# Down projections of four feed-forward blocks: first two weight tiles taken chunk by chunk together

## Chip, core and metric

The kernel runs on one core of a Trainium2 chip (trn2). The metric is device time in microseconds (us) of one execution, lower is better.

## What is computed

A two-layer transformer block with context tokens, followed by a second block. The change touches only the feed-forward part, which stands four times in the program (two layers, two halves each):

```python
def swiglu(x, w_gu, w_down):
    gt, up = jnp.split(x @ w_gu, 2, axis=-1)
    return (jax.nn.silu(gt) * up) @ w_down

def half_ffn(h, g, shift, scale, gate, w_gu, w_down):
    return h + 0.5 * gate * swiglu(norm_mod(h, g, shift, scale), w_gu, w_down)
```

The model width is 1024 and the feed-forward width 2816. There are 512 tokens and 256 context tokens; the first three feed-forward parts work on all 768, the last on 512.

## The kernel before

**Tiles.** Activations lie transposed, features on the 128 partitions and tokens along the free axis. A *tile* is 128 output features; a *chunk* is 128 input features of it. Every matrix product of the kernel is a *stage* of such tiles in one long list, numbered through (`plan`, L44). The weights of a tile come by DMA into one of four `raw` slots. ScalarE (ACT) rounds them to `wh` (`split_hi`, L309) and VectorE (DVE) writes the rest to `wl` (`split_lo`, L316). `wh` and `wl` have **two slots each**, taken in turn, so `split_hi` of tile n waits until TensorE (PE) has finished tile n-2:

```python
def w_slot_free(n):
    return n + 1
...
act.wait_ge(tile_done, w_slot_free(n))
```

The count `tile_done` stands at n+3 once tile n is done. A chunk is three products (high by high, high by low, low by high), each over 512 and then, with 768 tokens, 256 columns: six matmuls on L325, or three with 512 tokens. A tile has its own 1024 columns of PSUM, four of them in turn.

**A feed-forward part.** Its width is cut in two halves, a and b, of eleven 128-wide pieces. Each half is an *up* stage (22 tiles of 8 chunks: gate and up tiles in turn) and a *down* stage (8 tiles of 11 chunks). There are so eight down stages: four parts, halves a and b. For each pair of up tiles, ACT takes silu of the gate tile (L519), and DVE multiplies by the up tile (L546), rounds the product to `hidh` (L550) and writes the rest to `hidl` (L552), which raises `hid_done` by one. `hidh` and `hidl` piece q is what chunk q of the down stage streams.

**Order around a down stage.** Each engine has a program written out by hand. Let u be the last up tile, and d0 to d7 the down tiles.

- PE (`ffn_pe`, L502; `products`, L319): tiles of the up stage; a wait until `hid_done` has counted all eleven pieces (L507); then d0, d1, ... one after the other. Before each tile PE waits for its `wl` and for its PSUM (`weights`, L331).
- ACT (`act_tiles`, L355): in its turn for tile n it first splits the weights of tile n+1, then does its own work for tile n. In a down stage of half b that own work is the square of residual row n for the next norm (L415), which waits until DVE has added tile n to `h`.
- DVE (`dve_tiles`, L364): in its turn for tile n it first does `split_lo` of tile n+1, then its own work for tile n. In the turn of u that is L546, L550, L552. In the turns of the down stage it is the add of the tile to `h` (L394).

So both split engines handle d0's weights while u is multiplied, and d1's after u is done.

`products` already has a second way to begin a stage (`chunk_ready`, from L342): it waits for the weights of **both** first tiles, and then for each chunk q calls `chunk_ready(q)` and multiplies chunk q of the first tile and chunk q of the second. The stages that follow a norm are begun so, the up stages of half a and `ev_in` among them; they are called *head pairs* below.

Of the kernel before, what the change touches and what calls it, by code (L numbers as in the profile page):

```python
# [66 lines left out]
def build(nc, t):  # L67
# [9 lines left out]
    with ctx:  # L77
# [8 lines left out]
        def sb(name, at, shape, dt=f32):  # L86
            return nc.alloc_sbuf_tensor_at(name, [P] + list(shape), dt, offset=at)

        def words(*shape):
            return 4 * int(np.prod(shape))  # L90
# [49 lines left out]
        hidh = sb("hidh", R_AT, [JA, T], f32r)  # L140
        hidl = sb("hidl", R_AT + words(JA, T), [JA, T], f32r)
# [88 lines left out]
        def S(name):  # L230
            if name not in made:
                made[name] = ctx.enter_context(nc.semaphore(name))
            return made[name]
# [8 lines left out]
        def lo_ready(n):  # L242
            return n + 5
# [7 lines left out]
        def psum_free(n):  # L251
            return n + 1
# [9 lines left out]
        def segs(tokens):  # L262
            return [(0, TX)] if tokens == TX else [(0, TX), (TX, T)]
# [20 lines left out]
        def run_tiles(eng, stage, one, done=0):  # L284


            b = stage.first
            for k in range(done, stage.head):
                one(b + k, k, b + k, None)
            if stage.loops:  # L290
                with eng.Fori(0, stage.loops) as i:
                    for c in range(stage.head, stage.head + 4):
                        one(i * 4 + (b + c), i * 4 + c, b + c, i)
            for k in range(max(done, stage.head + 4 * stage.loops), stage.tiles):
                one(b + k, k, b + k, None)
# [23 lines left out]
        def products(pe, stage, xh, xl, chunk_ready=None, then=None):  # L319


            def chunk(c, q):
                for j, (w, x) in enumerate(((wh, xh), (wh, xl), (wl, xh))):
                    for s, e in segs(stage.tokens):
                        last = nc.tensor.matmul(  # L325
                            psum[:, (c % 4) * 1024 + s:(c % 4) * 1024 + e],
                            w[:, c % 2, q * P:(q + 1) * P], x[:, q, s:e],
                            start=(q == 0 and j == 0), stop=(q == stage.chunks - 1 and j == 2))
                return last

            def weights(n):  # L331
                pe.wait_ge(w_lo, lo_ready(n))
                pe.wait_ge(drained, psum_free(n))

            def one(n, k, c, i):
                weights(n)
                for q in range(stage.chunks):
                    last = chunk(c, q)
                last.then_inc(tile_done, 1)
                if then:  # L340
                    then(k)

            if chunk_ready:
                pair = (stage.first, stage.first + 1)
                for n in pair:
                    weights(n)
                for q in range(stage.chunks):
                    chunk_ready(q)
                    for n in pair:
                        last = chunk(n, q)  # L350
                        if q == stage.chunks - 1:
                            last.then_inc(tile_done, 1)
            run_tiles(pe, stage, one, done=2 if chunk_ready else 0)
# [79 lines left out]
        def norm_pe(pe, k, tokens):  # L433


            pe.wait_ge(n_add, KD * (k + 1))
            for a in range(tokens // P):
                last = nc.tensor.matmul(psum[:, NPS[k] + a:NPS[k] + a + 1], scr[:, SQ_ALL, a * P:(a + 1) * P],
                                        ones[:, 0:1], start=True, stop=True)
            last.then_inc(n_sum, 1)  # L440
            pe.wait_ge(n_r, k + 1)
            for a in range(tokens // P):
                last = nc.tensor.matmul(psum[:, NPS[k] + a * P:NPS[k] + (a + 1) * P],  # L443
                                        ncol[:, a:a + 1].to_broadcast([P, P]), ident[:], start=True, stop=True)
            last.then_inc(n_spr, 1)
# [33 lines left out]
        def after_norm(pe, k):  # L479
            return lambda q: pe.wait_ge(n_z, KD * k + q + 1)  # L480


        silu_done, hid_hi, hid_done = S("silu_done"), S("hid_hi"), S("hid_done")
# [9 lines left out]
        def ffn_parts(f):  # L493
            return [(ST[f"ffn{f}_up_a"], ST[f"ffn{f}_down_a"], f * NJ),
                    (ST[f"ffn{f}_up_b"], ST[f"ffn{f}_down_b"], f * NJ + JA)]
# [6 lines left out]
        def ffn_pe(pe, f):  # L502
            k = NORM_OF_FFN[f]
            norm_pe(pe, k, ffn_parts(f)[0][0].tokens)
            for up, down, pairs in ffn_parts(f):
                products(pe, up, zh, zl, after_norm(pe, k) if pairs == f * NJ else None)
                pe.wait_ge(hid_done, pairs + up.tiles // 2)  # L507
                products(pe, down, hidh, hidl)

        def ffn_act(act, f):  # L510
            k, layer, s = NORM_OF_FFN[f], f // 2, 2 * (f % 2)
# [1456 lines left out]
        @block.tensor  # L1968
        def _(pe):
            pe.sem_inc(tile_done, 2)  # L1970
            pe.sem_inc(drained, 4)
            start_pe(pe)
            ffn_pe(pe, 0)
            even_pe(pe)
            ffn_pe(pe, 1)
            ffn_pe(pe, 2)
            odd_pe(pe)
            ffn_pe(pe, 3)
            dn_pe(pe)
            swa_pe(pe)  # L1980
            tail_pe(pe)
# [143 lines left out]
```

## Time and profile before

| | us |
|---|---|
| median of 3 runs | 4123.52 (4123.34 to 4126.46) |
| span of the profiled execution, first to last instruction | 4120.1 |
| PE busy in it | 3838.0 (93%) |
| DVE busy | 1719.9 (42%) |
| ACT busy | 1130.2 (27%) |
| mean granted PE clock | 0.952 of full speed |

The profile gives one execution by its span; the time of that execution outside the span is not listed apart. The median of the runs is 3.4 us above the span. The granted clock is given as a share: 1.00 is 2.4 GHz and 0.50 is 1.2 GHz, and a value between them is a stretch that holds some of both. Matmuls of 512 and 256 columns that follow each other are merged in the timeline (x2).

### The profile page before, as it was taken

The page shows a single profiled execution, that of the slowest core. Times are in us where ns is not written, and L with a number is a line of the kernel's source. Part 1 is how long each engine was busy: PE and PEld are TensorE (multiplying, and loading weights), DVE is VectorE, ACT ScalarE, POOL GpSimd, SP SyncE. Part 2 cuts the span into 40 slices and gives each one's busy share as a digit, 9 for nine tenths or more (in the row PEclk, how much of TensorE's full clock was granted, in tenths as well). Part 3 has the DMA queues.
Part 4 walks back from the last instruction along what each step waited for, and adds up shares of the span by engine and source line. Part 5 has one row for each costly group of instructions (what it writes and reads, how often), then busy time and mean ns, then how long its engine had stood idle before and what let it go on. Part 6 is the DMA issues. An engine that isn't in the chain of part 4 may idle for free.

```text
span 4120.1 us, 48230 instructions
## 1 busy us (share of the span) xinstructions
PE 3838.0 (93%) x20346; PEld 3154.8 (77%) x20346; DVE 1719.9 (42%) x2308; ACT 1130.2 (27%) x1468; POOL 15.8 (0%) x33
## 2 busy tenths in 40 slices
PE   8999999998789999999999989999998978888898
PEld 3368888887677888887888878777887777666677
DVE  6853222333764222223322244564334654444434
ACT  6741111123443111113111131443223321222232
POOL 0000000000000000000000000000000000000000
PEclk9999999998899999999999999899999987999999
DMA  9931112110001111211211212012232200111122
GB/s 367 340 119 63 65 57 75 57 59 21 4 16 52 64 64 60 71 54 51 71 52 61 70 58 80 21 45 83 93 101 79 77 1 27 46 47 45 48 76 88
DMA packets 64686, 301.67 MB, mean 73 GB/s; under 512 B 7472, under 2 KB 7664, under 8 KB 59664
## 3 DMA queue, kind: packets, MB, share of 16 engines
q1 hardware_dynamic: 61776, 286.89, 20.4%
q0 software_dynamic: 2752, 12.49, 0.8%
q8 instruction: 122, 2.00, 0.2%
q14 instruction: 36, 0.29, 0.0%
HBM read 297.25 MB, written 2.10 MB: 73 GB/s over the span
## 4 chain that ended last, share of the span: by engine, by line
PE 86%; DVE 9%; ACT 3%; issue 2%; DMA 1%; DVEq 0%; POOL 0%; ACTq 0%; SPq 0%
PE psum L325 69%; PE psum L627 5%; PE psum L937 2%; PE psum L760 2%; PE psum L954 1%; PE psum L945 1%; DVE nmx L1001 1%; PE psum L773 1%; DMA adaw<-in_ada_w 1%; PE psum L1393 1%; ACT scr L454 0%; DVE ev_s L998 0%; PE psum L443 0%; PE psum L1402 0%; DVE wl L316 0%
## 5 line engine op out<-in xcount | busy, mean ns | idle before, releaser
L325 PE MATMUL psum<-zh,wh 128*128 128x512 f32 (+1 forms) x3728 | 1124.6, 358 | 64.9 <-DVE zl L473 29.2
L325 PE MATMUL psum<-zh,wl 128*128 128x512 f32 (+1 forms) x3728 | 1118.7, 357 | 0.0
L325 PE MATMUL psum<-zl,wh 128*128 128x512 f32 (+1 forms) x3728 | 1117.6, 357 | 0.0
L316 DVE TENSOR_TENSOR wl<-raw,wh 128x1024 fp32r<-128x1024 f32 (+2 forms) x383 | 485.6, 1268 | 653.1 <-ACT wh L309 652.3
L325 PEld LDWEIGHTS psum<-zh,wh 128*128 128x128 f32 x3728 | 617.4, 191 | 176.8 <-issue 41.7
L309 ACT ACTIVATE wh<-raw 128x1024 fp32r<-128x1024 f32 (+2 forms) x383 | 416.4, 1089 | 1075.1 <-PE psum L325 1073.5
L325 PEld LDWEIGHTS psum<-zh,wl 128*128 128x128 f32 x3728 | 616.6, 190 | 106.0
L325 PEld LDWEIGHTS psum<-zl,wh 128*128 128x128 f32 x3728 | 616.2, 191 | 102.3
L325 PE MATMUL psum<-hidh,wh 128*128 128x512 f32 x1232 | 342.1, 347 | 20.2 <-DVE hidl L552 20.2
L325 PE MATMUL psum<-hidl,wh 128*128 128x512 f32 x1232 | 342.9, 348 | 0.0
L325 PE MATMUL psum<-hidh,wl 128*128 128x512 f32 x1232 | 340.4, 346 | 0.0
L394 DVE SCALAR_TENSOR_TENSOR h<-psum,mod,h 128x512 f32<-128x512 f32 (+1 forms) x136 | 82.0, 637 | 507.1 <-PE psum L325 507.1
L546 DVE TENSOR_TENSOR scr<-scr,psum 128x768 f32<-128x768 f32 (+1 forms) x88 | 78.1, 887 | 400.5 <-PE psum L325 400.5
L325 PEld LDWEIGHTS psum<-hidh,wh 128*128 128x128 f32 x1232 | 195.2, 190 | 53.3 <-DVE hidl L552 23.0
L519 ACT ACTIVATE scr<-psum 128x768 f32<-128x768 f32 (+1 forms) x88 | 66.8, 759 | 578.5 <-PE psum L325 578.5
L325 PEld LDWEIGHTS psum<-hidh,wl 128*128 128x128 f32 x1232 | 196.3, 190 | 31.4
L325 PEld LDWEIGHTS psum<-hidl,wh 128*128 128x128 f32 x1232 | 196.4, 190 | 30.0
L673 DVE TENSOR_TENSOR adal<-adaw,adah 128x2048 fp32r<-128x2048 f32 x72 | 163.9, 2290 | 54.4 <-ACT adah L653 54.3
L653 ACT ACTIVATE adah<-adaw 128x2048 fp32r<-128x2048 f32 x72 | 137.1, 1908 | 41.6 <-PE psum L627 26.2
L415 ACT ACTIVATE scr<-h 128x768 f32<-128x768 f32 (+1 forms) x56 | 43.8, 783 | 380.1 <-DVE h L394 380.1
L627 PE MATMUL psum<-adah,scch 128*2 128x512 f32 x288 | 114.8, 399 | 17.5 <-DVE adal L673 17.5
L627 PE MATMUL psum<-adah,sccl 128*2 128x512 f32 x288 | 114.1, 396 | 0.0
(365 smaller groups left out, 3229.0 us busy)
## 6 DMA issues: line engine op xcount, KB each, us to landing
adaw<-in_ada_w SPq DMA_DIRECT2D x36, 2048.0 KB, 9.5
raw<-in_wup_a SPq DMA_DIRECT2D x88, 512.0 KB, 3.3
raw<-in_wup_b SPq DMA_DIRECT2D x88, 512.0 KB, 3.3
raw<-in_wdn_a SPq DMA_DIRECT2D x32, 704.0 KB, 4.0
raw<-in_wdn_b SPq DMA_DIRECT2D x32, 704.0 KB, 4.1
raw<-in_w_sw SPq DMA_DIRECT2D x36, 512.0 KB, 3.3
raw<-in_od_in SPq DMA_DIRECT2D x16, 512.0 KB, 3.3
raw<-in_w_ga SPq DMA_DIRECT2D x16, 512.0 KB, 3.3
```

What stands on the lines that cost most here:

```text
L309: nc.scalar.activation(wh[:, c % 2, 0:w], raw[:, c % 4, 0:w], ACT.Copy).then_inc(w_hi, 1)
L316: nc.vector.tensor_tensor(wl[:, c % 2, 0:w], raw[:, c % 4, 0:w], wh[:, c % 2, 0:w], ALU.subtract).then_inc(w_lo, 1)
L325: last = nc.tensor.matmul(psum[:, (c % 4) * 1024 + s:(c % 4) * 1024 + e], w[:, c % 2, q * P:(q + 1) * P], x[:, q, s:e], start=(q == 0 and ...
L394: last = nc.vector.scalar_tensor_tensor(h[:, k, s:e], a, col, h[:, k, s:e], ALU.mult, ALU.add)
L415: nc.scalar.activation(scr[:, c % 2, 0:tokens], h[:, c, 0:tokens], ACT.Square).then_inc(n_sq, 1)
L519: nc.scalar.activation(scr[:, (c - up.first) // 2 % 2, 0:tok], acc(c, tok), ACT.Silu).then_inc(silu_done, 1)
L546: nc.vector.tensor_tensor(p, scr[:, b:b + 1, 0:tok], acc(c, tok).rearrange("p (a n) -> p a n", a=1), ALU.mult).then_inc(drained, 2)
L627: last = nc.tensor.matmul(psum[0:2, i % 4 * 512:i % 4 * 512 + 512], x[:, q, :], w, start=q == 0 and n == 0, stop=q == KD - 1 and n == 2)
L653: nc.scalar.activation(adah[:, j % 3], adaw[:, i % 3, half], ACT.Copy).then_inc(ada_hi, 1)
L673: nc.vector.tensor_tensor(adal[j % 3][:], adaw[:, i % 3, half], adah[:, j % 3], ALU.subtract).then_inc(ada_lo, 1)
L760: last = nc.tensor.matmul(psum[:, c:c + gr.heads], gr.sq[:, it.k % 2, a * P:(a + 1) * P], gr.pick(), start=True, stop=True)
L937: last = nc.tensor.matmul(u.scores(c, w), q, k, start=True, stop=True)
```

## The change

Each down stage is begun as a head pair. The one wait for all eleven pieces is gone, and chunk q waits for piece q.

```diff
--- before.py
+++ after.py
@@ -504,8 +504,7 @@
             norm_pe(pe, k, ffn_parts(f)[0][0].tokens)
             for up, down, pairs in ffn_parts(f):
                 products(pe, up, zh, zl, after_norm(pe, k) if pairs == f * NJ else None)
-                pe.wait_ge(hid_done, pairs + up.tiles // 2)
-                products(pe, down, hidh, hidl)
+                products(pe, down, hidh, hidl, lambda q: pe.wait_ge(hid_done, pairs + q + 1))
 
         def ffn_act(act, f):
             k, layer, s = NORM_OF_FFN[f], f // 2, 2 * (f % 2)
```

Lines below this one move up by one: the `hidl` write is L552 before and L551 after.

PE's program at the end of tile d0 of the first down stage, before the change (66 matmuls stand between one wait for weights and the next):

```order
1508 L325 MATMUL psum<-hidh,wl 128x512
1509 L325 MATMUL psum<-hidh,wl 128x256
1510 L325 MATMUL psum<-hidh,wh 128x512 [waits drained,w_lo]
1511 L325 MATMUL psum<-hidh,wh 128x256
1512 L325 MATMUL psum<-hidl,wh 128x512
```

Behind d0's last chunk stands the wait for d1's `wl`. In the changed kernel that place (row 1510) is in the middle of the pair and has no wait. The waits for both tiles' weights stand at row 1444, and from there on every twelfth matmul waits for its piece; this is PE at the end of chunk 0 of d1:

```order
1454 L325 MATMUL psum<-hidh,wl 128x512
1455 L325 MATMUL psum<-hidh,wl 128x256
1456 L325 MATMUL psum<-hidh,wh 128x512 [waits hid_done]
1457 L325 MATMUL psum<-hidh,wh 128x256
1458 L325 MATMUL psum<-hidl,wh 128x512
```

Chunk 1 of d0 now follows chunk 0 of d1, and the last chunk of d0 stands one chunk before the end of the pair.

DVE's program around the same boundary is the same in both (this is the changed kernel):

```order
151 L316 TENSOR_TENSOR wl<-raw,wh 128x1408 [waits w_hi]
152 L545 TENSOR_TENSOR scr<-scr,psum 128x768 [waits silu_done,tile_done]
153 L549 CAST hidh<-scr 128x768 [waits drained]
154 L551 TENSOR_TENSOR hidl<-scr,hidh 128x768 [waits hid_hi]
155 L316 TENSOR_TENSOR wl<-raw,wh 128x1408 [waits w_hi]
156 L394 SCALAR_TENSOR_TENSOR h<-psum,mod,h 128x512 [waits tile_done]
157 L394 SCALAR_TENSOR_TENSOR h<-psum,mod,h 128x256
158 L316 TENSOR_TENSOR wl<-raw,wh 128x1408 [waits w_hi]
```

Row 151 is d0's `wl`, rows 152 to 154 the last piece of the hidden values, row 155 d1's `wl`, rows 156 and 157 the add of d0, row 158 d2's `wl`. ACT's program is unchanged too; in a down stage of half b (the first of them here) it is, in both kernels:

```order
196 L309 ACTIVATE wh<-raw 128x1408 [waits tile_done,raw_loaded0]
197 L309 ACTIVATE wh<-raw 128x1408 [waits tile_done,raw_loaded1]
198 L415 ACTIVATE scr<-h 128x768 [waits drained]
199 L309 ACTIVATE wh<-raw 128x1408 [waits tile_done,raw_loaded2]
200 L415 ACTIVATE scr<-h 128x768 [waits drained]
```

These are `wh` of d0, `wh` of d1, the square of row 0, `wh` of d2, the square of row 1.

## Rows read from the trace of the kernel before

**Rows 1.** The page: busy time and share of the engines, and the chain's shares.

```profile
PE 3838.0 (93%) x20346; PEld 3154.8 (77%) x20346; DVE 1719.9 (42%) x2308; ACT 1130.2 (27%) x1468; POOL 15.8 (0%) x33
...
PE 86%; DVE 9%; ACT 3%; issue 2%; DMA 1%; DVEq 0%; POOL 0%; ACTq 0%; SPq 0%
```

**Rows 2.** Waits: engine, line, waited for; us in total, times, longest.

```profile
PE psum L325 <- DVE hidl L552: 20.2, 8, 2.7
```

**Rows 3.** Timeline at the first down stage: start us, us, engine, line, operation, count.

```profile
442.71 0.95 DVE L546 TENSOR_TENSOR scr<-scr,psum 128x768 f32<-128x768 f32 x1 [4.64 <-PE psum L325]
442.71 1.38 ACT L309 ACTIVATE wh<-raw 128x1408 fp32r<-128x1408 f32 x1 [6.30 <-PE psum L325]
...
444.29 0.96 DVE L552 TENSOR_TENSOR hidl<-scr,hidh 128x768 fp32r<-128x768 f32 x1
445.17 1.62 DVE L316 TENSOR_TENSOR wl<-raw,wh 128x1408 fp32r<-128x1408 f32 x1
...
445.30 0.97 PE L325 MATMUL psum<-hidh,wh 128*128 128x512 f32 x2 [2.69 <-DVE hidl L552]
```

**Rows 4.** Timeline at the end of the head pair of ev_in.

```profile
850.63 2.03 ACT L309 ACTIVATE wh<-raw 128x1024 fp32r<-128x1024 f32 x2 [5.12 <-PE psum L325]
...
851.07 0.50 PE L325 MATMUL psum<-zh,wl 128*128 128x512 f32 x2
851.73 1.23 DVE L316 TENSOR_TENSOR wl<-raw,wh 128x1024 fp32r<-128x1024 f32 x1 [0.19 <-ACT wh L309]
...
853.09 0.49 PE L325 MATMUL psum<-zh,wh 128*128 128x512 f32 x1 [1.51 <-DVE wl L316]
```

**Rows 5.** Timeline in the first down stage of half a, d0 just done.

```profile
458.62 1.14 DVE L394 SCALAR_TENSOR_TENSOR h<-psum,mod,h 128x512 f32<-128x512 f32 x2 [11.83 <-PE psum L325]
...
458.68 1.38 ACT L309 ACTIVATE wh<-raw 128x1408 fp32r<-128x1408 f32 x1 [14.59 <-PE psum L325]
...
460.09 1.63 DVE L316 TENSOR_TENSOR wl<-raw,wh 128x1408 fp32r<-128x1408 f32 x1 [0.33 <-ACT wh L309]
```

**Rows 6.** Timeline in the first down stage of half b, d0 just done.

```profile
737.87 1.14 DVE L394 SCALAR_TENSOR_TENSOR h<-psum,mod,h 128x512 f32<-128x512 f32 x2 [12.00 <-PE psum L325]
...
739.04 0.84 ACT L415 ACTIVATE scr<-h 128x768 f32<-128x768 f32 x1 [15.87 <-DVE h L394]
...
739.79 1.36 ACT L309 ACTIVATE wh<-raw 128x1408 fp32r<-128x1408 f32 x1
...
741.19 1.63 DVE L316 TENSOR_TENSOR wl<-raw,wh 128x1408 fp32r<-128x1408 f32 x1 [2.18 <-ACT wh L309]
```

**Rows 7.** The same in the last down stage, 512 tokens, half b.

```profile
3113.34 0.75 DVE L394 SCALAR_TENSOR_TENSOR h<-psum,mod,h 128x512 f32<-128x512 f32 x1 [6.33 <-PE psum L325]
3116.06 1.63 DVE L316 TENSOR_TENSOR wl<-raw,wh 128x1408 fp32r<-128x1408 f32 x1 [1.97 <-ACT wh L309]
```

**Rows 8.** Windows of 3.4 us after PE's short gaps: busy (x), granted clock, DMA share, GB/s.

```profile
274.38:277.78 3.40, 3.40 (x11) 0.55 0.50 154
445.30:448.70 3.40, 3.40 (x11) 0.51 0.25 65
...
1760.84:1764.24 3.40, 3.40 (x19) 1.00 0.27 65
...
3105.53:3108.93 3.40, 3.40 (x15) 1.00 0.24 60
```

**Rows 9.** Windows around a long gap between two stages of 512 tokens.

```profile
3920.00:3924.05 4.05, 4.05 (x18) 1.00 0.00 0
3924.05:3927.92 3.87, 0.00 (x1) 0.88 0.01 2
3927.92:3933.80 5.88, 5.88 (x14) 0.50 0.50 161
```

**Rows 10.** Timeline of PE within a head pair; 265.72 begins a chunk.

```profile
265.37 0.51 PE L325 MATMUL psum<-zh,wl 128*128 128x512 f32 x2
265.72 0.52 PE L325 MATMUL psum<-zh,wh 128*128 128x512 f32 x2
```

## Prediction

> **What bounds the kernel now.** I read the page's busy times and the chain of work that ended last first. PE is busy 93% of the span and the chain is 86% PE [rows 1], so a microsecond in which PE stands still beside these stages is a microsecond of the result, and so is one in which its clock is halved. DVE at 42% and ACT at 27% have room on average; what counts is where they answer late. The list of waits then says what the removed wait is worth at most: PE stood 20.2 us in all before the eight down stages, released each time by the last write of `hidl` [rows 2]. The timeline of the first such place shows what else happens in that gap [rows 3]. The last up tile u is seen done at 442.71. DVE multiplies, rounds and writes the rest, done at 445.25, and PE starts at 445.30 after 2.69 us. ACT splits d1's weights from 442.71, because only then is their slot free, and DVE cannot write d1's `wl` before 445.17, since the three hidden operations stand ahead of it in its program.
>
> **The first gap: longer by one weight split.** The change removes the wait for the last piece, and puts in its place a wait for d1's `wl` before the first matmul of the pair. On DVE that write is behind the hidden values: it starts at 445.17 and takes 1.62 us [rows 3], to 446.79. PE follows a `wl` write by 0.12 us (852.96 to 853.09 [rows 4]), so it starts at 446.91, not 445.30: **+1.6 us** in place of any gain. The waits of the chunks for their own pieces never bind, because the last piece is there 1.6 us before PE starts; the 20.2 us stay. DVE's order and width are the same in all eight stages (1408 wide in each), so 8 x 1.6 = 12.9 us.
>
> **The second gap: new, behind the pair.** d2's weights need the slot of d0. Before, d0 ended a whole tile ahead of d1's end, 66 matmuls or 11.8 us at 3.40/19 = 0.179 us each [rows 8], which covers the split. Now d0 ends one chunk before d1. The head pair of `ev_in` shows this gap at 1024 columns [rows 4]: tile 0 seen done at 850.63, the last matmul over at 851.57 (0.94 to 1.0 us later), `wl` of the third tile at 852.96, PE on at 853.09, idle 1.51 us. A down tile is wider. After d0 is seen done, ACT starts 0.06 later and takes 1.38, and `wl` ends at 461.72, 3.10 after 458.62 [rows 5]; with 0.12 it is 3.22, less the 1.0 us of d1's last chunk: **2.2 us** in half a. In half b ACT has the square of row 0 ahead of d2's `wh`, and it waits for DVE's add: done at 737.87, square at 739.04, `wh` at 739.79, `wl` at 741.19 to 742.82 [rows 6]. That is 4.95 + 0.12 - 1.0 = **4.1 us**. Before, this chain lay under tile d1. With 512 tokens a chunk is three matmuls of 4.05/18 = 0.225 us [rows 9], so only about 0.64 us is covered: half b is (3117.69 - 3113.34) + 0.12 - 0.64 = 3.8 us [rows 7], and half a 3.22 - 0.64 = 2.6 us. Sum: 3 x 2.2 + 2.6 + 3 x 4.1 + 3.8 = 25.3 us. Tile d3 does not inherit it: its split needs d1, done before d2 starts, and has d2's own length for cover. Both engines have no more work than before, and DMA is not on this path.
>
> PE's idle time added: 12.9 + 25.3 = **38.2 us**.
>
> **The clock after a gap.** This I read by windows. In the 3.4 us after the gap at 445.30 the granted clock was 0.51 and 11 matmuls ran; after that at 1760.84 it was 1.00 and 19 ran [rows 8]. Such a low stretch costs 3.4 x (1 - 11/19) = 1.4 us by the count, 3.4 x 0.49 = 1.7 by the clock; I take 1.5. There are twelve gaps of 2.0 to 2.7 us between tile products (before the eight down stages and behind the head pairs of the four up stages); nine are followed by a low stretch, three by a clock of 1.00 (1760.84, 3105.53 and one more; first, last and two between in [rows 8]), and of the eight down stages five are low. So the kernel pays 5 x 1.5 = 7.5 us at these places now. A longer gap: the one of 3.87 us is followed by 5.88 us at 0.50 in which 14 matmuls ran [rows 9]; at 0.225 us they would take 3.15, so it cost 2.7 us. The changed kernel has 12 gaps of 3.6 to 4.3 us (the first gap grows from 2.69 to 4.3, with 512 tokens from 2.0 to 3.6; and the four second gaps of half b). No down stage of before has such a gap. Its price lies between 1.5 and 2.7 us; I take the middle, 2.1, since the nearest rows are one at each end. Four second gaps of 2.2 to 2.6 us pay 1.5 us in nine cases of twelve. That is 12 x 2.1 + 4 x 9/12 x 1.5 - 7.5 = **22.2 us**.
>
> The Trainium skill (TensorE: Matmul & The Clock Gate, section HAM oscillation — how this bites in real kernels) says that short bursts of matmuls with waits between them pay the fall of the clock at each wait anew. By that rule, taken strictly, each of my sixteen gaps would pay, and the four at 9/12 would add 1.5 us in all; the trace shows three of twelve short gaps that did not.
>
> **Sum.** 4120.1 + 38.2 + 22.2 = 4180.5 us of span. The median of the runs stands 3.4 us above the span of the profiled execution, and I add that: **4184 us**, about 1.5% more than 4123.5. The idle part is firm to some 2 us. The clock part is, with 1.5 for each long gap and none for the four short ones, 10.5 us, and with 2.7 and all four, 30.9 us. So the forecast's own range is 4170 to 4195.
>
> **Rivals.**
>
> *Weight loads come into the open.* Each chunk's first matmul now waits on a count, 10 more of them in each stage, 80 in all. The Trainium skill (TensorE: Matmul & The Clock Gate, section Step-by-step: what each phase is for) says that weight loads are pulled ahead of running matmuls. If a wait stopped that, a load of 3154.8/20346 = 0.155 us [rows 1] would lie bare at each, 12 us, and the time would be 4196. Against it: in a head pair, which has the same waits, two matmuls start every 0.35 us, at a chunk's start as well [rows 10], as in a stretch without waits (3.40/19 x 2 = 0.36) [rows 8].
>
> *Only the first gap grows.* If d0's completion came early enough for the second gap to hide, only 12.9 us and about 10 us of clock would be left: 4146. For it speaks nothing but that ACT and DVE are idle then; `ev_in` shows the opposite, with a narrower split [rows 4].
>
> *Only the second gap counts,* if DVE wrote d1's `wl` ahead of the hidden values. Then the first gap keeps its length and the time is near 4123.5 + 25.3 + 12 = 4161. The timeline's order speaks against it.
>
> *Faster.* One mechanism would do it: the splits of d1 and of d2 run ahead of PE, as if the weights had a slot more. It decides at the slot: if d1's split starts 1.38 + 1.62 + 0.12 = 3.1 us before u is done [rows 3, 4], and d2's before d0 is, the first gap is gone with its clock, -20.2 - 7.5 = -28 us, and the time is 4096. ACT started d1's split at 442.71, the same instant at which DVE saw u done [rows 3], so the slot binds.
>
> *The change does not do what it says.* It does begin the stages in pairs; but the wait for each chunk's own piece is covered by the later wait for weights. This is part of the forecast. The pairing would be without effect only if both gaps were hidden: 4124.
>
> **Chances.** The forecast 0.86; loads in the open 0.04; first gap only 0.04; second gap only 0.04; faster 0.01; no effect 0.01. The range of 8 in 10 is 4167 to 4200. It takes in the clock's two prices, the 2 us of the idle part and the loads in the open. About 0.2% (8 us) is what a measurement of this kernel can tell from no change; faster by more than that 0.01, within it 0.01, slower 0.98.
>
> **What would show it.** In the changed profile PE should wait for no `hidl` at all at the eight down stages, but for DVE's `wl` L316, eight times 4.3 us (3.6 with 512 tokens). Sixteen waits of PE on `wl` should be new. Behind each pair, 22 to 24 us after its start (15 with 512 tokens), PE should stand 2.2 us in half a and 4.1 in half b, and in half b the chain should run through the add L394, the square L415, `wh` and `wl`. The mean clock should fall below 0.952, and the busy time of DVE and ACT should stay. I am wrong if PE starts the pair as `hidl` is done, if there is no gap behind the pair, or if the clock's part is outside 10 to 31 us.

## Result and the profile after

The changed kernel takes 4195.2 us (median of 4 runs, 4190.0 to 4200.1) where the kernel before takes 4125.0 beside it: a ratio of 1.018, with a 95% interval of 1.016 to 1.020. Forecast were 4184 us and a range of 4167 to 4200. A later comparison on another occasion (`after_again`, below) gave 1.016 (1.012 to 1.019); two of the 17 runs of the kernel before in that later comparison took 7.7 and 13.8 ms, and no median or ratio here counts them. The profiled execution has a span of 4198.3 us, 78.2 more than the 4120.1 of before, at a mean granted clock of 0.944 (0.952 before).

The page of the changed kernel; beside [rows 1] PE's busy time has grown by 42 us though it runs the same 20346 matmuls, and DVE and ACT are as they were:

```profile
PE 3880.2 (92%) x20346; PEld 3185.5 (76%) x20346; DVE 1719.2 (41%) x2308; ACT 1129.5 (27%) x1468; POOL 15.8 (0%) x33
```

The waits of PE. No wait for `hidl` is left (20.2 us in [rows 2]). The wait for `wl` stood in 14 places before:

```profile
PE psum L325 <- DVE wl L316: 23.6, 14, 5.5
```

It has sixteen places more now:

```profile
PE psum L325 <- DVE wl L316: 81.3, 30, 4.8
```

The chain at the first down stage. The `hidl` write now is followed by d1's `wl`, and PE starts when that is done, 4.38 us after it stopped (2.69 in [rows 3]):

```profile
445.57 0.97 DVE scr L545
...
446.56 0.57 DVE hidh L549
...
447.16 0.96 DVE hidl L551
448.12 1.54 DVE wl L316
449.66 0.20 issue
449.86 2.26 PE psum L325 x6
```

The chain behind the pair in a half a, a gap of the kind that `ev_in` had in [rows 4]: d2's `wh` as soon as d0 is done, then d2's `wl`, then PE.

```profile
474.55 1.39 ACT wh L309
...
475.96 1.64 DVE wl L316
...
477.64 1.56 PE psum L325 x7
```

And in a half b, with the add (L394) ahead of ACT's square (L415), and `wh` and `wl` behind it:

```profile
765.17 1.15 DVE h L394 x2
...
766.35 0.02 ACT scr L415
766.37 0.73 issue
767.10 1.37 ACT wh L309
...
768.49 1.64 DVE wl L316
770.13 0.04 issue
770.17 1.01 PE psum L325 x2
```

Windows of the three gaps, of what follows them, and of one long gap in the last part (busy, count, granted clock, DMA share, GB/s). They answer to [rows 8] and [rows 9]:

```profile
445.48:449.86 4.38, 0.00 (x0) 0.84 0.01 2
449.86:455.31 5.45, 5.45 (x17) 0.50 0.40 132
475.49:477.64 2.15, 0.00 (x0) 1.00 0.00 0
477.64:481.04 3.40, 3.40 (x15) 0.73 0.67 210
766.19:770.17 3.98, 0.00 (x1) 0.90 0.00 0
770.17:776.16 5.99, 5.99 (x19) 0.50 0.47 134
2979.33:2983.04 3.71, 0.00 (x0) 1.00 0.37 147
2983.04:2986.44 3.40, 3.40 (x15) 1.00 0.63 212
```

The gap before a stage is 4.38 us five times and 4.41 once in the parts of 768 tokens, and 3.7 twice with 512. Behind the pair it is 2.15 three times and 2.5 in half a, and 4.0 three times and 3.75 in half b.

**Where the 78 us are.** I take each of the four feed-forward parts from the end of its first up stage to the end of its last down stage. In the first part that is 442.61 to 819.45 before and 445.48 to 841.82 after, 19.5 us more; the others give 20.4, 13.4 and 15.0, in sum 68.3 us. Of these 38.2 us are idle time. The other 30.1 are, by the windows and the experiments below, the lower clock, 20.7 us, and a slower pace of the products, 7.9 us; 1.5 us stay without a cause. Ten us lie outside these four stretches: 2.9 up to the first down stage, whose up stage ran at the slower pace, some 2.6 between the parts and just behind the last, and 4.3 behind 3188 us in the second block. There PE is busy 4.5 us longer with the same work, at a mean granted clock of 0.91 where it was 0.92, and idle no longer than before; why the clock was lower there stays open.

### The profile page after: what moved, and what is told of

The parts are those of the page before. It is cut to its first block, busy times and chain, and to the rows that moved or that the text cites. A ratio compares the mean times of both kernels' runs of the same rounds, so it can differ in the third digit from the quotient of the medians.

```text
span 4198.3 us, 48230 instructions
## 1 busy us (share of the span) xinstructions
PE 3880.2 (92%) x20346; PEld 3185.5 (76%) x20346; DVE 1719.2 (41%) x2308; ACT 1129.5 (27%) x1468; POOL 15.8 (0%) x33
## 4 chain that ended last, share of the span: by engine, by line
PE 85%; DVE 9%; ACT 3%; issue 2%; DMA 1%; DVEq 0%; ACTq 0%; POOL 0%; SPq 0%
PE psum L325 68%; PE psum L626 4%; PE psum L936 2%; PE psum L759 2%; PE psum L953 1%; PE psum L944 1%; DVE nmx L1000 1%; DVE wl L316 1%; PE psum L772 1%; DMA adaw<-in_ada_w 1%; PE psum L1392 1%; ACT wh L309 1%; ACT scr L454 0%; DVE ev_s L997 0%; PE psum L443 0%
## 5 line engine op out<-in xcount | busy, mean ns | idle before, releaser
L325 PE MATMUL psum<-zh,wh 128*128 128x512 f32 (+1 forms) x3728 | 1130.2, 360 | 64.2 <-DVE zl L473 29.2
L325 PE MATMUL psum<-hidh,wh 128*128 128x512 f32 x1232 | 352.2, 356 | 58.5 <-DVE wl L316 58.5
L325 PE MATMUL psum<-hidh,wl 128*128 128x512 f32 x1232 | 348.9, 353 | 0.0
L394 DVE SCALAR_TENSOR_TENSOR h<-psum,mod,h 128x512 f32<-128x512 f32 (+1 forms) x136 | 82.0, 637 | 571.4 <-PE psum L325 571.4
L415 ACT ACTIVATE scr<-h 128x768 f32<-128x768 f32 (+1 forms) x56 | 43.8, 783 | 415.9 <-DVE h L394 415.9
```

What stands on the lines that cost most here:

```text
L325: last = nc.tensor.matmul(psum[:, (c % 4) * 1024 + s:(c % 4) * 1024 + e], w[:, c % 2, q * P:(q + 1) * P], x[:, q, s:e], start=(q == 0 and ...
L394: last = nc.vector.scalar_tensor_tensor(h[:, k, s:e], a, col, h[:, k, s:e], ALU.mult, ALU.add)
L415: nc.scalar.activation(scr[:, c % 2, 0:tokens], h[:, c, 0:tokens], ACT.Square).then_inc(n_sq, 1)
```

## Experiments

Each ratio is to the kernel before, run beside it on the same chip, with its 95% interval. 1% is 41 us. An edit is shown against the changed kernel, the first one against the kernel before.

**Chunk waits alone.** Twice, under two labels. A new argument of `products` calls the wait in the first tile of a stage that is not a pair:

```diff
             def one(n, k, c, i):
                 weights(n)
                 for q in range(stage.chunks):
+                    if piece and i is None and k == 0:
+                        piece(q)
                     last = chunk(c, q)
...
-                pe.wait_ge(hid_done, pairs + up.tiles // 2)
-                products(pe, down, hidh, hidl)
+                products(pe, down, hidh, hidl, piece=lambda q: pe.wait_ge(hid_done, pairs + q + 1))
```

> Chunk waits alone, tiles one after the other as before the change. Theory (a pair is what costs, chunk waits are harmless): d0's weights are ready 4 us before the last up tile ends and pieces 0 to 9 are done, so the eight gaps of 2.0 to 2.7 us (20.2 us) go, with the 7.5 us that the clock lost after five of them: about 4125 - 28 = 4097 us, PE waits for hidl 0 us. Rival 1 (a wait in front of a chunk bares a weight load of 0.155 us, 88 times): 4111. Rival 2 (the last piece binds in any order): 4125.

Measured: 0.992 (0.989 to 0.995), 4093.3 us beside 4121.8. That is 28.5 us less by the medians and 34 by the ratio (22 to 47). PE goes from the up stage into the down stage without a stop:

```profile
445.78 0.51 PE L325 MATMUL psum<-zh,wl 128*128 128x512 f32 x2
446.12 0.51 PE L325 MATMUL psum<-hidh,wh 128*128 128x512 f32 x2
446.48 0.53 PE L325 MATMUL psum<-hidl,wh 128*128 128x512 f32 x2
```

All eight gaps are gone with the low clock behind them, and the size fits the theory. The pair is the cost of the change; the chunk waits are its better half, and 88 of them bare no weight load. The stretch that begins at 273.80 in `chunk_again` (see the pace, below) has 22 of these waits in it and still ran at the faster of the two paces, 534.33 us for 3072 products; 22 bare loads of 0.155 us would have added 3.4. The Trainium skill (TensorE: Matmul & The Clock Gate, Step-by-step: what each phase is for) has the weight loads pulled ahead of running matmuls; by these numbers that holds across a wait that is already met.

> The kernel with chunk waits alone once more, timed beside the others. Theory: about 28 us under before (ratio 0.993), with no gap at the eight down stages; its three stretches of 3072 products draw their pace anew, each worth 10 us, so single runs spread over some 30 us. Rival (the pace of this kernel is fixed at 0.353): the three stretches are at 0.353 again and the spread is under 10 us.

Measured: 0.991 (0.989 to 0.994), 4090.4 us beside 4124.7, 34 us less; single runs from 4067.4 to 4096.6. The eight gaps are absent again, and one of the three long stretches ran at the faster pace, where in the first trace of this kernel none did.

**The pair with one wait.**

```diff
-                products(pe, down, hidh, hidl, lambda q: pe.wait_ge(hid_done, pairs + q + 1))
+                products(pe, down, hidh, hidl, lambda q: pe.wait_ge(hid_done, pairs + up.tiles // 2) if q == 0 else None)
```

> The pair, with one wait for all eleven pieces ahead of it. Theory: the wait for d1's wl ends 1.6 us after the last piece, so the chunk waits do nothing: same time as the changed kernel, 4195 us within 8. Rival (the chunk waits save part of the gap, which would be longer without them, or cost weight loads): 4210 or more, or 4183 or less.

Measured: 1.015 (1.010 to 1.019), 63.8 us over before, and PE waits 81.0 us for `wl` in 30 places and never for `hidl`, as in the changed kernel. The chunk waits do nothing behind a pair that waits for d1's weights.

**d0 done six chunks early.** The steps of a pair are written out, and the two tiles part before the end:

```diff
+                lead = stage.chunks - ahead
+                steps = [(q, n) for q in range(lead) for n in pair] + [(q, n) for n in pair for q in range(lead, stage.chunks)]
+                for q, n in steps:
+                    if n == pair[0]:
+                        chunk_ready(q)
+                    last = chunk(n, q)
+                    if q == stage.chunks - 1:
+                        last.then_inc(tile_done, 1)
```

Down stages take ahead=6; with the default of 1 the head pairs are as they were.

> The pair is interleaved for its first 5 chunks only; then d0's last 6 and then d1's last 6, so d0 ends six chunks (6.2 us, 4.1 with 512 tokens) before d1. Theory: the second gap (24.7 us in all) goes with its low clock (some 12 us), the first gap stays at 4.4 us: about 4195 - 37 = 4158 us, still slower than before by 33. Rival (the second gap has another cause, as the add to h or the next tile's transfer): 4190 or more.

Measured: 1.005 (1.003 to 1.007), 4145.4 beside 4121.8. In the profile every gap behind a down pair is gone and those ahead of the stages stay (4.38 to 4.41, and 3.7). Against `pair_one_wait` (63.8 us over before, in the same comparison) the second gap was worth some 40 us, where 37 were expected, and the first some 24. That the second is the slot's release is shown by both: the edit moved only the moment at which d0 ends, and the chains above go from that moment to d2's `wh` and `wl` and so to PE (in half b by way of the add and the square, see `square_late`).

**Filling the first gap of the pair.** PE multiplies d0's first chunks while it waits for d1's weights, each as a product of its own that the real one overwrites:

```diff
                 for n in pair:
                     weights(n)
+                    if fill and n == pair[0]:
+                        for q in range(fill):
+                            chunk(n, q, alone=True)
```

> While PE waits for d1's weights it multiplies d0's first 4 chunks (5 with 512 tokens) into the same PSUM, to be overwritten: 4.2 us of work in a wait of 4.4. Output unchanged. Theory (the low clock after the first gap is a cost of its own, about 2.1 us each): the clock stays at 1.00 after it, -17 us, about 4178 us. Rival 1 (the clock is no part of it): 4195. Rival 2 (the filling runs past the wait): 4200.

Measured: 1.010 (1.007 to 1.013), 4169.0 beside 4121.8; 16.6 us under `pair_one_wait` of the same comparison, where 17 were expected. The wait ended within 0.2 us of where it did, and the clock stays up from the stretch before to well behind it (windows, as above; the same at all eight stages):

```profile
444.00:449.00 5.00, 4.94 (x29) 1.00 0.17 41
449.00:455.00 6.00, 6.00 (x37) 1.00 0.22 90
```

Behind its gap the changed kernel ran 17 matmuls in 5.45 us, this one 37 in 6.00. Only the filling differs from the changed kernel, so the low clock after a gap is shown to be a cost of its own. The size is less firm: the 95% intervals of the two ratios just overlap. The two profiled spans are 8.4 us apart (4180.6 and 4172.2), and 2680 more products of the filled one ran at the slower pace (below), 8.8 us: without the pace it is 17.2.

**Filling the gap of the kernel before.**

```diff
                 weights(n)
+                if fill and i is None and k == 0:
+                    for q in range(2):
+                        chunk(c, q, alone=True)
+                    fill()
```

> The kernel before, with d0's first 2 chunks multiplied into their PSUM and overwritten, between the wait for d0's weights and the wait for all eleven pieces: 2.1 us of work (1.4 with 512 tokens) in a wait of 2.7 (2.0). Output unchanged. Theory: the wait ends when it did, and the clock stays up at all eight stages: -7.5 us against before. Rival (a short gap's low clock is chance and costs nothing on average): 0. The draw of the pace (see below, 0.347 or 0.353 us for two products) moves either by some 5 us.

Measured: 0.997 (0.995 to 0.999), 4113.8 beside 4129.2; by the ratio 13 us less, with an interval of 5 to 21. The 7.5 us at which I priced the five low stretches lie inside it, and no low stretch is left at any of the eight stages, where 0.6 us of idle time stays of each gap. PE does 2 us of useless work per stage here (1.4 with 512 tokens) and the kernel is faster for it.

**The order on DVE.** d1's `wl` ahead of the last `hidl` write, once with chunk waits and once with one wait:

```diff
+                    if i is None and j == up.tiles - 1:
+                        split_lo(dve, n + 2, c + 2, None)
                     dve.wait_ge(hid_hi, pair + 1)
                     nc.vector.tensor_tensor(ol, p, oh, ALU.subtract).then_inc(hid_done, 1)
```

(and the down stage's first turn no longer does that split).

> The changed kernel, with DVE's write of d1's wl moved ahead of the last hidl write (after the multiply and the rounding). Theory (the first gap ends with d1's wl, in DVE's order): wl starts as the rounding ends, 1.55 us after u, takes 1.62, so the gap is 3.4 us instead of 4.4 (3.3 instead of 3.7 with 512 tokens), -6.8 us in all and perhaps 2 of clock; the last piece comes 0.9 us after PE has started, and only the chunk waits allow that. Rival (PE cannot start before the last piece): the gap stays 4.3, 0 us.

Measured: 1.010 (1.008 to 1.012), 4164.1 beside 4124.7. The chain at the first down stage; PE starts with the last piece not yet written (it is done at 448.02):

```profile
445.06 0.56 DVE hidh L549
445.62 1.55 DVE wl L316
447.17 0.20 issue
447.37 2.04 PE psum L325 x5
```

The gap is 3.39 us six times and 3.34 twice, as expected. The time was not: some 9 us less than the changed kernel were expected, and the ratios say 24 to 33. In the traces, with the slower pace taken off, the spans differ by 18 and 22 us. The gaps are 6.7 of that. Most of the rest is clock: the mean granted clock is 0.947 here and 0.944 and 0.945 in the two traces of the changed kernel. Not all of it lies behind these gaps, and why there is less low clock elsewhere stays open.

> split_first with one wait for all pieces ahead of the pair. Theory: PE starts when hidl is done, 4.3 us after u: time of the changed kernel, about 8 us over split_first. Rival (chunk waits have no value in any order): the time of split_first.

Measured: 1.013 (1.011 to 1.016), 4179.8 beside 4124.7. PE starts only behind `hidl`, with a gap of 4.19:

```profile
443.77 1.53 DVE wl L316
445.31 0.88 DVE hidl L553
446.19 0.14 issue
446.32 0.76 PE psum L325
```

The two gaps show that chunk waits pay in a pair only if DVE's order puts the weights first. The gaps differ by 5.9 us in all (0.8 six times and 0.54 twice), the medians by 15.7 and the profiled spans by 14.9 (4166.2 and 4181.1). In the traces 1716 more products of `split_first_one` ran at the slower pace, 5.7 us; without it 9.2 are left, where 8 were expected.

**The square one turn later.**

```diff
+                def square_before(n, c, _, i):
+                    if c >= 1:
+                        act.wait_ge(drained, n + 4)
+                        square(act, k + 1, c - 1, tok)
+                act_tiles(act, down, None if first else square_before)
```

(and the last square behind the stage).

> The changed kernel, with ACT's square of a residual row one turn later in the down stages of half b, so that d2's wh no longer stands behind the add to h and the square. Theory (that chain is what makes the second gap 4.0 us in half b instead of 2.2): it falls to 2.2 us (2.5 with 512 tokens), -6.8 us and some 3 of clock, about 10 us less than the changed kernel. Rival (the slot alone, or the wait of PE for drained PSUM): the gap stays 4.0, 0 us.

Measured: 1.015 (1.012 to 1.017), 4177.9 beside 4124.7. The chain behind the first pair of a half b has lost the add and the square:

```profile
761.47 1.39 ACT wh L309
762.86 0.02 issue
762.88 1.64 DVE wl L316
764.52 0.04 issue
764.56 1.86 PE psum L325 x5
```

The gap is 2.13 us there, and 2.15, 2.16 and 2.51 in the others, as expected. The time against the changed kernel's 1.016 to 1.018 is 4 to 14 us less, around the 10 expected; it proves no size.

**Chunk waits, and the head pairs parted.** `chunk_only` with the steps of `pair_early`, ahead=3 in every head pair:

> chunk_only, and in every head pair (up stages of half a, ev_in, od_in_x, dn_in) the first tile's last 3 chunks ahead of the second tile's last 3. Theory (the gap behind a pair is the slot's, as after the change): the gaps of 1.5 to 2.3 us behind the seven pairs shrink to under 1 us, some 11 us, and the low clock after four of them goes, 6 us: about 17 us less than chunk_only, some 4077 where before is 4122. Rival (the norm's values come late, and the order costs at the front what it gives behind): the time of chunk_only.

Measured: 0.990 (0.987 to 0.993), 4089.0 us beside 4129.2. The gaps behind the head pairs of the up stages, `ev_in` and `od_in_x` are gone: no stop of over 1.5 us stands there. Against `chunk_only` at 0.992 and 0.991, 17 us were expected; by the ratios it is some 6, and not even that is shown, as the intervals overlap. The rival has a part in it: PE waits 12.6 us for `wl` where it was 24.3 in `chunk_only`, but 31.7 for the norm's `zl` where it was 29.2, and in `od_in_x` two stops of 1.16 and 1.10 us for `zl` replace the one of 1.77. Both beat the kernel before and the changed one.

**The changed kernel and the kernel before, once more.**

> The changed kernel once more, to see whether its product pace is drawn anew in each execution. Theory (each stretch between two gaps draws 0.347 or 0.353 us for two products, whatever the order): the gaps stay 4.4 / 3.7 and 2.2 / 2.5 / 4.0 us, some stretches change their pace, and the time is 4185 to 4200. Rival (the change itself sets the slow pace behind a pair of half a): the three long stretches behind the pairs of half a are at 0.353 again.

Measured: 1.016 (1.012 to 1.019), 4193.1 us (4184.1 to 4198.7), span of the profile 4182.3.

> The kernel before once more. Theory (draw): gaps of 2.7 and 2.0 us as before, other stretches at 0.353 than in the first trace, span 4110 to 4140. Rival (the pace belongs to the place in the program): the same stretches at 0.353, those begun at 724, 853, 1307, 2058 and 2468 us.

Measured: one run of 4135.3 us, span 4133.5.

**The pace.** These two runs are about it. The chain merges the products of a stretch without a stop (start, us, count). Stretches of 1584 in the first trace of before:

```profile
445.30 276.40 PE psum L325 x1584
...
1481.74 276.42 PE psum L325 x1584
...
2058.98 281.65 PE psum L325 x1584
```

In `before_again`, the same places:

```profile
448.19 281.64 PE psum L325 x1584
...
1489.42 276.41 PE psum L325 x1584
...
2071.90 281.63 PE psum L325 x1584
```

The same work takes 276.4 or 281.6 us and nothing between: 0.0033 us per product. The clock is not the cause: each of the six begins with one low stretch of the same length, and behind it the clock is 1.00. A window of the first stretch in the first trace of before has 579 matmuls at that clock:

```profile
560.00:660.00 100.00, 100.00 (x579) 1.00 0.19 63
```

The same window in `before_again` has 568:

```profile
560.00:660.00 100.00, 100.00 (x568) 1.00 0.19 63
```

The place does not decide it, since the first stretch has changed. Behind the pairs of half a the changed kernel had the slower pace three times (258.3 less a low stretch of 1.5, and 256.8 without one), while `after_again` had

```profile
474.99 256.80 PE psum L325 x1452
...
1526.80 253.57 PE psum L325 x1452
...
2120.65 253.56 PE psum L325 x1452
```

(once slow; the two others are at the faster pace with a low stretch each). So the rival that the pair sets the slow pace falls. In `chunk_again` the stretches are 3072 long, and one draw is worth 10.2 us:

```profile
273.80 534.33 PE psum L325 x3072
1294.66 544.52 PE psum L325 x3072
1872.29 542.99 PE psum L325 x3072
```

(The third had no low stretch.) Three draws of 10.2 us would make up the 29 us over which the runs of this kernel spread; the runs without a trace do not show it. Two traces of one kernel do: 4224 products of 768-token stages ran at the slower pace in the first trace of before and 8112 in `before_again`, 12.8 us by 0.0033 each, and the spans differ by 13.4. What decides the draw stays open.

## Why the prediction was right, point by point

**What bounds.** PE, with the clock: right. Every edit that lengthened, shortened or filled a gap of PE moved the time. The pace of the products moved it too, without any gap; the prediction did not know of it.

**The first gap, +1.6 us each.** Right. It measured 4.38 (predicted 4.3) and 3.7 (3.6); in sum 33.8 us where 20.2 stood, +13.5 against 12.9 predicted. The step on which it rests, DVE's order, is shown by `split_first`; that chunk waits never bind here, by `pair_one_wait`.

**The second gap, 2.2 and 4.1 us.** Right in mechanism and size: 2.15 and 4.0, with 512 tokens 2.5 and 3.75 (2.6 and 3.8). Sum 24.7 us against 25.3. `pair_early` shows the slot and `square_late` the chain of half b. The place was a little off: the gap came 24.5 to 25.9 us after the pair's start (15.3 and 16.8 with 512 tokens), not 22 to 24 (15), because a low clock at the start of the pair lies on top of its 132 products.

**The clock, 22.2 us.** Right as a sum, rough in its parts. I read 6.2 us behind each of the twelve long gaps. One minus the granted clock, summed over the twelve, is 4.10, times 6.2 us is 25.4 us of lost clock. At 0.50 two products start every 0.64 us (17 in 5.45) instead of 0.347, which loses 0.46 of the time and so 0.92 of the lost clock: 23.4 us, or 1.95 for a gap where I had 2.1. Three of the four short second gaps have 0.72 in the same window, 1.7 x 3 x 0.92 = 4.8 us (4.5 predicted). With the 7.5 us of before taken off it is 20.7 us. That the sum came so near is in part luck, as its parts scatter. The bounds for one long gap, 1.5 and 2.7, did not hold: the gap of 3.71 us at 2979 cost nothing (clock 1.00 behind it), while that at 770 cost 5.99 x 0.5 x 0.92 = 2.8. By the Trainium skill's rule on waits between bursts (TensorE: Matmul & The Clock Gate, HAM oscillation — how this bites in real kernels), each wait pays the fall anew; here 14 of 16 did. `pair_fill` shows that this term exists, at some 17 us for the first gaps.

**The sum.** 38.2 us of idle time were predicted and 38.2 came. The four parts grew by 68.3 us where 60.4 were expected, and my sum had no term for the pace, which is 7.9 us. 2112 products of these parts ran at the slower pace in the first trace of before and 4488 in that of after (three stretches of 1452 and one pair of 132): 2376 x 0.0033 = 7.9 us. (The clock's 20.7 is 1.5 under its forecast, and 1.5 us have no cause found.) The pace is luck of the two traces and not the change. Over the whole traces 7560 products were slow after and 4224 before, 11.0 us of the 78.2; in `after_again` and `before_again` 3912 and 8112, which hides 13.9 us behind spans 48.8 apart. Without the pace the change is 67 and 63 us. The medians differ by 70, 64 and, in the equal kernel `pair_one_wait`, 64 us: all a little over the 60 of the forecast, which knew of nothing outside the four parts. The measured 4195.2 stands at the upper end of the forecast's own 4170 to 4195 and inside 4167 to 4200. That range had no width for the pace, and so was right by less margin than it seemed.

**The rivals.** Loads in the open: refuted by `chunk_only`. First gap only, second gap only, no effect: refuted by the profile, which has both gaps. Faster, by a slot more: not tried, as SBUF would have to be laid out anew; but the 28 us that it named are got in another way by `chunk_only` (28 to 34 measured), which lets d0 run alone while d1 is split.

## What to carry to other kernels

A finer wait is worth what the next coarser wait behind it leaves: here the chunk waits were worth 28 to 34 us alone and nothing behind a wait for the second tile's weights. Interleaving two tiles needs both tiles' buffers at the start and gives both back at the end, so with two slots it opens a gap on either side; where it is needed for another reason, let the first tile finish some chunks early. And a gap of PE costs more than its own length: those of 3.7 to 4.4 us cost about 2 us of low clock each on top, eleven of twelve paying, and those of 2.0 to 2.7 us about 1.5 us in three cases of four; so the gaps of an engine at 93% are to be counted one by one.

## What was unexpected of the hardware

In these traces a 512-column and a 256-column product together took one of two paces, 0.347 or 0.353 us, at a full clock, and held it over a whole stretch without a stop, of up to 3072 products; the next stretch may have the other. It can move a run by some 30 us where the stretches are long. Stages of 512 tokens showed a single pace (264 products of a down stage took 60.15 us in the first trace of before and 60.16 in `before_again`). And useless matmuls in a gap of PE made the kernel before faster by 13 us (5 to 21); the idle wait ended where it did, and what changed in the trace is the clock.
